# Decode and prompt tails of a one-core decoder step: rounding of the first chunk weights and merge weight steps moved in the written order

## The chip, the cores and the metric

The kernel runs on one core of a Trainium2 chip. The metric is the device time of one execution in microseconds. The engines are TensorE (PE; its weight loads are listed as PEld), VectorE (DVE), ScalarE (ACT), GpSimd (POOL) and SyncE (SP), which issues DMAs. They run side by side and wait for each other through semaphores. A "stage" of this kernel ends with a barrier of all engines.

## What is computed

One layer of a hybrid decoder, on a prompt of 256 tokens and on 8 sequences that decode 4 tokens each over a paged cache of 2048 rows. Cut to what matters here:

```
z   = RMSNorm(x) @ w_in                      # q, k, v, forget, branch gates, merge gates
NSA = gate_c * compressed(MLP of 32-row chunks) + gate_s * selected blocks + gate_w * window
FoX = softmax(q k + sum of log forget gates) v
h   = x + W_out( sigmoid(gA) * (W_oA NSA) + sigmoid(gB) * (W_oB FoX) )
y   = h + W_down( gelu(conv3(RMSNorm(h) W_up)) * (RMSNorm(h) W_gate) )
```

The chunk MLP needs weights `cmp_w1` (for k and v); the merge needs the gate columns gA and gB of `w_in`, in 8 groups of 128 columns, and `w_o`.

## The kernel before

All of it is float32. The large products are made of three passes with rounded halves: a "high" half, written by ScalarE (`split_high`, L249), a "low" half, the rest, written by VectorE (`split_low`, L254), and then high*high, low*high, high*low on TensorE (L261 to L263). A split is thus a ScalarE copy, then a VectorE subtraction that waits for it, then the products.

The stages in order are tokens, projection, prompt attention, compress (chunk MLP), decode, merge and FFN. Two places matter.

**The tail of the prompt stage** (`stage_prompt`, L752). Twelve units (four of selected and four of window attention, in turns, then four of FoX; U = 12) pass through scores, exponentials, `turn` (transposes of the probabilities, L902), copies out of PSUM (`take_turned`, VectorE L1029 for the first tile and ScalarE L960 for the second) and `values` (L925). `values(m)` waits for both copies of unit m, and for a FoX unit also for ScalarE's copy of the rows before it (`fox_rows_out`, L968). The loops run with lags: `turn` two steps and `values` three steps behind the scores. In this tail the kernel also prepares the next stage: TensorE transposes the first chunk rows (`chunks.turn(0, ...)`, L1105), ScalarE writes the high half of the first two eighths of the k chunk weights (`first_weights`), and VectorE their low halves, behind its last copy.

**The end of the decode stage** (`stage_decode`, L1573). The order of all work is one list of steps, `decode_steps()`, written out by hand; every engine runs through the same list and does what each step has for it. A `vals` step of job fox multiplies one block of gathered value rows (L1902, 8 products of 512 columns), one of job nsa the selected values of one sequence (L1868, L1871); `fold` sums slots (L1878 and L1907), `merge` scales them on VectorE (ending with L2147 for nsa, L2157 for fox), `out` transposes the result (L1764) and VectorE takes it (L2179, L2174). The rows come from the paged cache through GpSimd's indirect DMAs into a ring of 8 slots; a slot's next gather waits until its last user is done. Between these stand steps for the merge stage, which would have nothing else to wait for:

- `split(n)`: the halves of merge weights, n = 0 and 1 for the gate column groups `gates1` and `gates`, n = 2 for `w_o`.
- `branch(i)`: the halves of the prompt's NSA and FoX rows.
- `gates(n, x)`: the products of gate group n for branch x, 24 products of 288 columns (L261 to L263). `gates(0, x)` write PSUM banks 0 and 1, `gates(1, 0)` bank 4, which FoX logits used, `gates(1, 1)` bank 5, which holds the NSA sums until their merge.

When `gates(0, 1)` is done, GpSimd issues the load of a third gate group into the place of `gates1`, and ScalarE rounds it after its list. SyncE loads `w_o` when the last user of ring slot 5, the selected values of sequence 2, is done.

In the prompt stage this work is placed so:

```
if n == U + T_LAG - 1:                     # PE, n = 13: before turn(11)
    pe.wait_ge(neg, 4 * U)
...
    chunks.turn(0, lambda k, x: c.ps[x])
if n >= U + PV_LAG - EARLY:                # ACT, n = 13 and 14, last in each round
    first_weights(n - U - PV_LAG + EARLY)
for q in range(EARLY):                     # DVE, behind its loop
    dve.wait_ge(w_high, q + 1)
```

Of the kernel before, what the change touches and what calls it, by code (L numbers as in the profile page):

```python
# [751 lines left out]
def stage_prompt(c, z, chunks):  # L752


    nc, d = c.nc, c.d
# [4 lines left out]
    with c.stage() as ctx:  # L760
# [109 lines left out]
        def _(pe):  # L870
# [58 lines left out]
            for n in range(U + PV_LAG):  # L929
                if n < U:  # L930
                    scores(n)
                if n == 1:
                    cumulate()
                if n == T_LAG:
                    pe.wait_ge(cum_out, 2)
                if n == U + T_LAG - 1:
                    pe.wait_ge(neg, 4 * U)
                    for b in range(2):
                        pe.wait_ge(chunks.raw_in[b], 16)
                    chunks.turn(0, lambda k, x: c.ps[x])  # L940
                if T_LAG <= n < U + T_LAG:
                    turn(n - T_LAG)
                if n >= PV_LAG:
                    values(n - PV_LAG)

        @block.scalar
        def _(act):
# [25 lines left out]
            for n in range(U + PV_LAG):  # L973
                if n < U:
                    exponentials(n)
                if T_LAG <= n < U + T_LAG:
                    take_turned(n - T_LAG)
                if n >= N + PV_LAG:
                    fox_rows_out(n - N - PV_LAG)
                if n >= U + PV_LAG - EARLY:  # L980
                    first_weights(n - U - PV_LAG + EARLY)

        @block.vector
        def _(dve):
# [40 lines left out]
            def take_turned(m):  # L1025
# [2 lines left out]
                    dve.wait_ge(pv, m - 1)  # L1028
                nc.vector.tensor_copy(pT[m % 2][:, :, 0, :], c.ps[3][:, 0:2 * P].rearrange("p (j n) -> p j n", j=2)).then_inc(copied[0], 1)  # L1029

            def nsa_rows_out(r):
                dve.wait_ge(pv, 2 * r + 2)
                to = slice(r % 2 * HD, (r % 2 + 1) * HD)
# [5 lines left out]
            for n in range(U + T_LAG):  # L1039
# [4 lines left out]
                if n == 1:  # L1044
                    dve.wait_ge(cum_ready, 1)
                    nc.vector.tensor_copy(cq[:, :, :], c.ps[3][:, 0:2 * NH].rearrange("p (t h) -> p t h", t=QT)).then_inc(cum_out, 1)
                    nc.vector.tensor_scalar(neg_cq[:, :, :], c.ps[3][:, 0:2 * NH].rearrange("p (t h) -> p t h", t=QT), -1.0, None, ALU.mult).then_inc(cum_out, 1)
                if n >= T_LAG:
                    take_turned(n - T_LAG)
                if 1 <= n <= U:  # L1050
                    shares(n - 1)
                    normalise(n - 1)
                if 4 <= n < 4 + N and n % 2 == 0:
                    nsa_rows_out((n - 4) // 2)
            for q in range(EARLY):
                dve.wait_ge(w_high, q + 1)
                split_low(nc, chunks.eighths(chunks.w1l[0], q), chunks.eighths(chunks.w1[0], q), chunks.eighths(chunks.w1h, q))


ND = DB * NCH  # L1060
# [73 lines left out]
EARLY = 2  # L1134
# [343 lines left out]
def decode_steps():  # L1478
# [30 lines left out]
              + fold("fox", 0, 3) + select(1, 5))  # L1509
    end = (vals(1, 0) + merge("fox", 0) + probs(1, 3, 4) + nsa(1, 1) + out("fox", 0) + vals(1, 1) + probs(1, 0) + nsa(1, 2) + vals(1, 2) + nsa(1, 3) + vals(1, 3)  # L1510
           + nsa(1, 4) + vals(1, 4) + fold("fox", 1, 0) + nsa_probs(1, 0, 1) + vals(1, 5) + exps("sel", 1, 0, 1, 2) + nsa_probs(1, 2) + vals(1, 6) + exps("sel", 1, 3, 4)
           + nsa_probs(1, 3, 4) + vals(1, 7) + nsa_probs(1, 5, 6) + vals(1, 8) + fold("fox", 1, 1) + nsa_probs(1, 7) + branch(0) + nsa_vals(1, 0) + vals(1, 9)
           + split(0) + branch(1) + nsa_vals(1, 1) + vals(1, 10) + nsa_vals(1, 2) + gates(0, 0) + vals(1, 11) + nsa_vals(1, 3) + fold("nsa", 1, 0) + merge("nsa", 1)
           + gates(0, 1) + vals(1, 12) + out("nsa", 1) + fold("fox", 1, 2) + vals(1, 13) + split(1) + vals(1, 14) + gates(1, 0) + vals(1, 15) + fold("fox", 1, 3) + merge("fox", 1)
           + split(2) + gates(1, 1) + out("fox", 1))
    return start + middle + end


# [1444 lines left out]
```

## Time and profile before

| | |
|---|---|
| median of 3 runs | 906.74 us (906.27 to 909.92) |
| the profiled execution | 905.39 us, of which the span of the trace is 903.3 us |
| PE busy | 832.6 us, 92% of the span |
| DVE, ACT, POOL busy | 509.8 us (56%), 366.7 us (41%), 177.9 us (20%) |
| mean granted TensorE clock | 0.969 |
| HBM traffic | 188.09 MB read, 7.64 MB written |
| prompt stage ends, compress starts | 163.9 us, 164.7 us |
| decode ends, merge starts | 548.6 us, 549.5 us |

The busy shares are averages over stages with different limits. In the chain that ended last nearly all is TensorE (products of L261 to L263), since the last stage is bound by it; it doesn't tell what holds the earlier stages, for which the timelines are read.

### The profile page before, as it was taken

The page shows a single profiled execution, that of the slowest core. Times are in us where ns is not written, and L with a number is a line of the kernel's source. Part 1 is how long each engine was busy: PE and PEld are TensorE (multiplying, and loading weights), DVE is VectorE, ACT ScalarE, POOL GpSimd, SP SyncE. Part 2 cuts the span into 40 slices and gives each one's busy share as a digit, 9 for nine tenths or more (in the row PEclk, how much of TensorE's full clock was granted, in tenths as well). Part 3 has the DMA queues.
Part 4 walks back from the last instruction along what each step waited for, and adds up shares of the span by engine and source line. Part 5 has one row for each costly group of instructions (what it writes and reads, how often), then busy time and mean ns, then how long its engine had stood idle before and what let it go on. Part 6 is the DMA issues. An engine that isn't in the chain of part 4 may idle for free. (4 is left out here: it accounts for less than half of the span.)

```text
span 903.3 us, 18508 instructions
## 1 busy us (share of the span) xinstructions
PE 832.6 (92%) x7475; PEld 685.2 (76%) x7475; DVE 509.8 (56%) x970; ACT 366.7 (41%) x660; POOL 177.9 (20%) x274
## 2 busy tenths in 40 slices
PE   3899888899999999999998688999889999999997
PEld 3899756789889876656554357996589889989885
DVE  5477568433435677734566335646656655656654
ACT  4346655433334244632234403535154334444432
POOL 1000177200230033343443510000011100101100
PEclk9999869999999999999999899999989999999999
DMA  6453196752236299999999996954064445554412
GB/s 216 151 173 141 32 302 245 146 193 95 95 137 232 100 402 358 329 391 408 419 416 396 400 342 182 267 208 153 1 233 140 141 139 174 191 188 143 139 46 62
DMA packets 90785, 192.57 MB, mean 213 GB/s; under 512 B 7482, under 2 KB 68826, under 8 KB 78202
## 3 DMA queue, kind: packets, MB, share of 16 engines
q1 hardware_dynamic: 75020, 84.57, 30.4%
q0 software_dynamic: 15408, 106.04, 30.4%
q8 instruction: 51, 0.84, 0.4%
q10 hardware_dynamic: 288, 0.97, 0.3%
q14 instruction: 18, 0.15, 0.0%
HBM read 188.09 MB, written 7.64 MB: 217 GB/s over the span
## 5 line engine op out<-in xcount | busy, mean ns | idle before, releaser
L1729 PEld LDWEIGHTS banks<-consts_base,stream_rows 128*128 128x128 f32 x672 | 73.2, 141 | 33.9 <-issue 26.9
L1968 ACT ACTIVATE keys_turned<-banks 128x512 f32<-128x512 f32 x94 | 55.0, 597 | 98.2 <-PE banks L1729 90.9
L261 PE MATMUL banks<-tokens_turned_high,w_gates_high 128*128 128x288 f32 x288 | 86.6, 301 | 3.5 <-PEq L194 2.3
L1729 PE MATMUL banks<-consts_base,stream_rows 128*128 128x128 f32 x672 | 82.7, 276 | 7.4 <-DVE fox_probs_turned L1959 2.6
L262 PE MATMUL banks<-tokens_turned_low,w_gates_high 128*128 128x288 f32 x288 | 85.4, 297 | 0.0
L263 PE MATMUL banks<-tokens_turned_high,w_gates_low 128*128 128x288 f32 x272 | 81.8, 301 | 0.0
L1262 PE MATMUL banks<-chunks_turned_high,cmp_w_high 64*128 64x256 f32 (+1 forms) x512 | 77.2, 295 | 2.6 <-ACT cmp_hidden L1356 2.6
L1262 PE MATMUL banks<-chunks_turned_low,cmp_w_high 64*128 64x256 f32 (+1 forms) x512 | 73.9, 282 | 0.0
L1949 DVE COPY keys_turned<-banks 128x512 f32<-128x512 f32 x74 | 50.3, 690 | 32.9 <-PE banks L1729 28.2
L254 DVE TENSOR_TENSOR chunks_turned_low<-banks,chunks_turned_high 128x512 fp32r<-128x512 f32 x64 | 41.1, 685 | 41.2 <-ACT chunks_turned_high L249 41.2
L249 ACT ACTIVATE chunks_turned_high<-banks 128x512 fp32r<-128x512 f32 x64 | 34.8, 596 | 67.8 <-PE banks L1105 65.7
L261 PEld LDWEIGHTS banks<-tokens_turned_high,w_gates_high 128*128 128x128 f32 x288 | 55.3, 192 | 6.1 <-issue 3.5
L261 PE MATMUL banks<-tokens_turned_high,w_up_gate_high 128*128 128x288 f32 x192 | 58.0, 302 | 0.0
L263 PE MATMUL banks<-tokens_turned_high,w_up_gate_low 128*128 128x288 f32 x192 | 57.1, 297 | 0.0
L1262 PEld LDWEIGHTS banks<-chunks_turned_high,cmp_w_high 64*128 64x128 f32 x512 | 49.4, 187 | 9.7 <-issue 6.1
L262 PE MATMUL banks<-tokens_turned_low,w_up_gate_high 128*128 128x288 f32 x192 | 56.7, 295 | 0.0
L262 PEld LDWEIGHTS banks<-tokens_turned_low,w_gates_high 128*128 128x128 f32 x288 | 55.7, 194 | 0.4
L2784 POOL COPY conv_new_state<-up_turned 128x2 f32 (+1 forms) x24 | 16.4, 684 | 200.5 <-ACT up_turned L2750 200.5
L263 PEld LDWEIGHTS banks<-tokens_turned_high,w_gates_low 128*128 128x128 f32 x272 | 52.0, 191 | 0.0
L1262 PEld LDWEIGHTS banks<-chunks_turned_low,cmp_w_high 64*128 64x128 f32 x512 | 49.5, 187 | 0.0
L1564 POOL DMA_INDIRECT stream_rows<-in_cache_fox_k,fox_row x32 | 30.8, 963 | 87.9 <-PE banks L1729 39.6
L261 PE MATMUL banks<-w_in_high,tokens_turned_high 128*128 128x356 f32 x128 | 43.6, 341 | 3.3 <-DVE w_in_low L254 3.3
(454 smaller groups left out, 2096.4 us busy)
## 6 DMA issues: line engine op xcount, KB each, us to landing
w_up_gate<-in_w_up SPq DMA_DIRECT2D x12, 1024.0 KB, 7.5
w_up_gate<-in_w_gate SPq DMA_DIRECT2D x12, 1024.0 KB, 9.9
w_down<-in_w_down SPq DMA_DIRECT2D x12, 1024.0 KB, 5.1
w_in_slot<-in_w_in SPq DMA_DIRECT2D x7, 1424.0 KB, 7.3
w_gates<-in_w_in SPq DMA_DIRECT2D x10, 512.0 KB, 7.1
cmp_w_k<-in_cmp_w_k SPq DMA_DIRECT2D x4, 512.0 KB
cmp_w_v<-in_cmp_w_v SPq DMA_DIRECT2D x4, 512.0 KB
stream_rows<-in_state_win_k SPq DMA_DIRECT2D x8, 256.0 KB, 8.0
```

What stands on the lines that cost most here:

```text
L249: return nc.scalar.activation(high, x, ACT.Copy)
L254: return nc.vector.tensor_tensor(low, x, high.bitcast(F32), ALU.subtract)
L261: nc.tensor.matmul(out, lh, rh, start=start, stop=False, **kw)
L262: nc.tensor.matmul(out, lh, rl, start=False, stop=False, **kw)
L263: return nc.tensor.matmul(out, ll, rh, start=False, stop=stop, **kw)
L1262: ins = nc.tensor.matmul(c.ps[4 + g][:, 0:w], x[rows, half * CS + 4 * q + i, :], y[k % 2][rows, i, src], start=(q + i + half + part == 0), ...
L1564: c.nc.gpsimd.indirect_dma_start(c.stream[r][:, :], None, table, bass.IndirectOffsetOnAxis(ap=rows, axis=0)).then_inc(c.ring_in[r], 16)
L1729: ins = nc.tensor.transpose(bank(t)[:, q * P:(q + 1) * P], src, ident)
L1949: copy(kT[kbuf[step]][:, x, :], bank(t)).then_inc(copied[e], 1)
L1968: copy = lambda a, b: nc.scalar.activation(a, b, ACT.Copy)
L2784: nc.gpsimd.tensor_copy(dst[:, :, 0:2], ue[f][:, SEQ:SEQ + 2].unsqueeze(1))
```

## The change

The change moves work in the written order; no instruction is added or taken away. In the prompt stage ScalarE's two high halves of chunk weights move one and two rounds up, ahead of its copies; VectorE's two low halves go around its last copy out of PSUM instead of behind it; TensorE's transposes of the first chunk rows go from before `turn(11)` to between `values(10)` and `values(11)`. In the decode list, `split(0)` and `split(1)` come before `branch(0)` and `branch(1)`, the four `gates` steps move up between the value steps (two of them by three value steps, the last ahead of the last three FoX value blocks), and `split(2)` comes behind the last merge.

```diff
--- before.py
+++ after.py
@@ -933,13 +933,13 @@
                     cumulate()
                 if n == T_LAG:
                     pe.wait_ge(cum_out, 2)
-                if n == U + T_LAG - 1:
+                if T_LAG <= n < U + T_LAG:
+                    turn(n - T_LAG)
+                if n == U + PV_LAG - 1:
                     pe.wait_ge(neg, 4 * U)
                     for b in range(2):
                         pe.wait_ge(chunks.raw_in[b], 16)
                     chunks.turn(0, lambda k, x: c.ps[x])
-                if T_LAG <= n < U + T_LAG:
-                    turn(n - T_LAG)
                 if n >= PV_LAG:
                     values(n - PV_LAG)
 
@@ -977,8 +977,8 @@
                     take_turned(n - T_LAG)
                 if n >= N + PV_LAG:
                     fox_rows_out(n - N - PV_LAG)
-                if n >= U + PV_LAG - EARLY:
-                    first_weights(n - U - PV_LAG + EARLY)
+                if U <= n < U + EARLY:
+                    first_weights(n - U)
 
         @block.vector
         def _(dve):
@@ -1028,6 +1028,10 @@
                     dve.wait_ge(pv, m - 1)
                 nc.vector.tensor_copy(pT[m % 2][:, :, 0, :], c.ps[3][:, 0:2 * P].rearrange("p (j n) -> p j n", j=2)).then_inc(copied[0], 1)
 
+            def low_weights(q):
+                dve.wait_ge(w_high, q + 1)
+                split_low(nc, chunks.eighths(chunks.w1l[0], q), chunks.eighths(chunks.w1[0], q), chunks.eighths(chunks.w1h, q))
+
             def nsa_rows_out(r):
                 dve.wait_ge(pv, 2 * r + 2)
                 to = slice(r % 2 * HD, (r % 2 + 1) * HD)
@@ -1045,16 +1049,17 @@
                     dve.wait_ge(cum_ready, 1)
                     nc.vector.tensor_copy(cq[:, :, :], c.ps[3][:, 0:2 * NH].rearrange("p (t h) -> p t h", t=QT)).then_inc(cum_out, 1)
                     nc.vector.tensor_scalar(neg_cq[:, :, :], c.ps[3][:, 0:2 * NH].rearrange("p (t h) -> p t h", t=QT), -1.0, None, ALU.mult).then_inc(cum_out, 1)
+                if n == U + T_LAG - 1:
+                    low_weights(0)
                 if n >= T_LAG:
                     take_turned(n - T_LAG)
+                if n == U + T_LAG - 1:
+                    low_weights(1)
                 if 1 <= n <= U:
                     shares(n - 1)
                     normalise(n - 1)
                 if 4 <= n < 4 + N and n % 2 == 0:
                     nsa_rows_out((n - 4) // 2)
-            for q in range(EARLY):
-                dve.wait_ge(w_high, q + 1)
-                split_low(nc, chunks.eighths(chunks.w1l[0], q), chunks.eighths(chunks.w1[0], q), chunks.eighths(chunks.w1h, q))
 
 
 ND = DB * NCH
@@ -1509,10 +1514,10 @@
               + fold("fox", 0, 3) + select(1, 5))
     end = (vals(1, 0) + merge("fox", 0) + probs(1, 3, 4) + nsa(1, 1) + out("fox", 0) + vals(1, 1) + probs(1, 0) + nsa(1, 2) + vals(1, 2) + nsa(1, 3) + vals(1, 3)
            + nsa(1, 4) + vals(1, 4) + fold("fox", 1, 0) + nsa_probs(1, 0, 1) + vals(1, 5) + exps("sel", 1, 0, 1, 2) + nsa_probs(1, 2) + vals(1, 6) + exps("sel", 1, 3, 4)
-           + nsa_probs(1, 3, 4) + vals(1, 7) + nsa_probs(1, 5, 6) + vals(1, 8) + fold("fox", 1, 1) + nsa_probs(1, 7) + branch(0) + nsa_vals(1, 0) + vals(1, 9)
-           + split(0) + branch(1) + nsa_vals(1, 1) + vals(1, 10) + nsa_vals(1, 2) + gates(0, 0) + vals(1, 11) + nsa_vals(1, 3) + fold("nsa", 1, 0) + merge("nsa", 1)
-           + gates(0, 1) + vals(1, 12) + out("nsa", 1) + fold("fox", 1, 2) + vals(1, 13) + split(1) + vals(1, 14) + gates(1, 0) + vals(1, 15) + fold("fox", 1, 3) + merge("fox", 1)
-           + split(2) + gates(1, 1) + out("fox", 1))
+           + nsa_probs(1, 3, 4) + vals(1, 7) + nsa_probs(1, 5, 6) + vals(1, 8) + fold("fox", 1, 1) + nsa_probs(1, 7) + split(0) + nsa_vals(1, 0) + split(1) + vals(1, 9)
+           + gates(0, 0) + branch(0) + nsa_vals(1, 1) + vals(1, 10) + gates(0, 1) + branch(1) + nsa_vals(1, 2) + gates(1, 0) + vals(1, 11) + nsa_vals(1, 3) + fold("nsa", 1, 0)
+           + merge("nsa", 1) + vals(1, 12) + out("nsa", 1) + fold("fox", 1, 2) + gates(1, 1) + vals(1, 13) + vals(1, 14) + vals(1, 15) + fold("fox", 1, 3)
+           + merge("fox", 1) + split(2) + out("fox", 1))
     return start + middle + end
 
 
```

ScalarE, tail of the prompt stage (`prompt_probs_turned` is the copy of a unit's turned probabilities, `h_rows` the copy of a finished row pair, `cmp_w_high` the weight half). Before:

```order
L968 ACTIVATE h_rows<-banks 128x256
L960 ACTIVATE prompt_probs_turned<-banks 128x2x256
L968 ACTIVATE h_rows<-banks 128x256
L249 ACTIVATE cmp_w_high<-cmp_w_k 128x2x512
L968 ACTIVATE h_rows<-banks 128x256
L249 ACTIVATE cmp_w_high<-cmp_w_k 128x2x512
```

and with the change:

```order
L968 ACTIVATE h_rows<-banks 128x256
L249 ACTIVATE cmp_w_high<-cmp_w_k 128x2x512
L960 ACTIVATE prompt_probs_turned<-banks 128x2x256
L968 ACTIVATE h_rows<-banks 128x256
L249 ACTIVATE cmp_w_high<-cmp_w_k 128x2x512
L968 ACTIVATE h_rows<-banks 128x256
```

Both weight halves moved up by one copy or two; a row copy is now the engine's last work of the stage.

VectorE, the same tail, before and with the change:

```order
L1013 RECIPROCAL prompt_sums<-prompt_sums 128x4
L1023 TENSOR_TENSOR prompt_logits<-prompt_logits,prompt_sums 128x2x128
L1023 TENSOR_TENSOR prompt_logits<-prompt_logits,prompt_sums 128x2x256
L1029 COPY prompt_probs_turned<-banks 128x2x128
L254 TENSOR_TENSOR cmp_w_low_k<-cmp_w_k,cmp_w_high 128x2x512 x2
```

```order
L1013 RECIPROCAL prompt_sums<-prompt_sums 128x4
L1023 TENSOR_TENSOR prompt_logits<-prompt_logits,prompt_sums 128x2x128
L1023 TENSOR_TENSOR prompt_logits<-prompt_logits,prompt_sums 128x2x256
L254 TENSOR_TENSOR cmp_w_low_k<-cmp_w_k,cmp_w_high 128x2x512
L1029 COPY prompt_probs_turned<-banks 128x2x128
L254 TENSOR_TENSOR cmp_w_low_k<-cmp_w_k,cmp_w_high 128x2x512
```

The last copy out of PSUM, for which `values(11)` waits, now stands behind one of the two low halves.

TensorE, end of the decode, from the selected values of sequence 0 on (L1871 before and L1876 after are selected values, L1902 and L1907 a FoX value block, L261 and so on the gate products), before and with the change:

```order
L1871 MATMUL banks<-stream_rows,sel_logits 32x128 x16
L1902 MATMUL banks<-stream_rows,fox_probs_turned 32x512 x4
L1868 MATMUL banks<-sample_rows_kept,nsa_probs_turned 32x128
L1871 MATMUL banks<-stream_rows,sel_logits 32x128 x16
L1902 MATMUL banks<-stream_rows_66,fox_probs_turned 32x512 x4
L1868 MATMUL banks<-sample_rows_kept,nsa_probs_turned 32x128
L1871 MATMUL banks<-stream_rows_67,sel_logits 32x128 x16
L261 MATMUL banks<-tokens_turned_high,w_gates_high_early 128x288
```

```order
L1876 MATMUL banks<-stream_rows,sel_logits 32x128 x16
L1907 MATMUL banks<-stream_rows,fox_probs_turned 32x512 x4
L261 MATMUL banks<-tokens_turned_high,w_gates_high_early 128x288
L262 MATMUL banks<-tokens_turned_low,w_gates_high_early 128x288
L263 MATMUL banks<-tokens_turned_high,w_gates_low_early 128x288
```

The first 24 gate products now follow the FoX block that comes before the selected values of sequence 1; before, the first of them came after the selected values of sequence 2.

## Rows read from the trace of the kernel before

**Rows 1.** Timeline, VectorE, 155 to 164: start us, us, engine, line, op, operands, idle before

```profile
158.62 0.42 DVE L1029 COPY prompt_probs_turned<-banks 128x256 f32<-128x256 f32 x1 [0.99 <-PE banks L902]
...
162.63 1.23 DVE L254 TENSOR_TENSOR cmp_w_low_k<-cmp_w_k,cmp_w_high 128x1024 fp32r<-128x1024 f32 x1 [0.17 <-ACT cmp_w_high L249]
```

**Rows 2.** Timeline, ScalarE, the same stretch

```profile
157.39 0.39 ACT L968 ACTIVATE h_rows<-banks 128x256 f32<-128x256 f32 x1 [0.22 <-PE banks L925]
...
160.15 1.05 ACT L249 ACTIVATE cmp_w_high<-cmp_w_k 128x1024 fp32r<-128x1024 f32 x1
```

**Rows 3.** Timeline, TensorE, the same stretch

```profile
157.27 1.09 PE L1105 MATMUL banks<-consts_base,stream_rows 128*128 128x128 f32 x8
...
158.20 0.82 PE L902 MATMUL banks<-consts_base,prompt_logits 128*128 128x128 f32 x6
...
160.36 0.88 PE L925 MATMUL banks<-prompt_probs_turned,z 128*64 128x128 f32 x12 [0.53 <-issue]
```

**Rows 4.** Stretches: us; busy PE, PEld, DVE, ACT, POOL; clock, DMA share, GB/s

```profile
110.00:120.00 10.00, 7.63 (x36) 4.75 (x33) 6.00 (x37) 6.08 (x25) 7.91 (x9) 0.50 1.17 194
161.30:164.70 3.40, 0.00 (x0) 0.00 (x0) 2.39 (x2) 1.30 (x2) 0.00 (x0) 1.00 0.00 0
164.70:168.40 3.70, 3.63 (x26) 3.33 (x28) 2.58 (x4) 2.17 (x4) 1.63 (x9) 0.56 0.63 175
168.40:172.10 3.70, 3.70 (x50) 3.38 (x50) 0.00 (x0) 0.41 (x1) 0.57 (x2) 0.98 1.04 279
478.00:480.40 2.40, 0.14 (x2) 0.00 (x0) 2.26 (x7) 0.34 (x1) 0.00 (x0) 1.00 1.02 427
516.30:520.10 3.80, 3.57 (x42) 1.95 (x42) 0.29 (x1) 0.00 (x0) 0.94 (x1) 0.50 1.03 425
550.30:554.20 3.90, 3.76 (x17) 3.79 (x18) 2.20 (x1) 1.69 (x3) 0.18 (x1) 0.57 0.84 264
```

**Rows 5.** Timeline, TensorE, from 510 us to the end of the decode

```profile
510.35 1.07 PE L1902 MATMUL banks<-stream_rows,fox_probs_turned 128*32 128x512 f32 x8 [0.29 <-DMA stream_rows<-in_cache_fox_v,fox_row]
...
516.35 0.39 PE L1868 MATMUL banks<-sample_rows_kept,nsa_probs_turned 128*32 128x128 f32 x1 [4.93 <-DMA stream_rows<-in_cache_sel_v,eighth_row]
...
518.84 1.67 PE L1902 MATMUL banks<-stream_rows,fox_probs_turned 128*32 128x512 f32 x8 [0.18 <-DMA stream_rows<-in_cache_fox_v,fox_row]
...
521.32 0.27 PE L1868 MATMUL banks<-sample_rows_kept,nsa_probs_turned 128*32 128x128 f32 x1 [0.81 <-DMA stream_rows<-in_cache_sel_v,eighth_row]
...
528.53 0.43 PE L1878 MATMUL banks<-nsa_slot_sums,consts_base 128*32 128x128 f32 x8 [0.50 <-DVE nsa_slot_sums L2132]
...
537.51 0.40 PE L261 MATMUL banks<-tokens_turned_high,w_gates_high 128*128 128x288 f32 x1 [1.20 <-DVE w_gates_low_in_place L254]
...
542.76 1.04 PE L1907 MATMUL banks<-fox_slot_sums,consts_base 128*32 128x512 f32 x2 [0.81 <-DVE fox_slot_sums L2164]
...
547.02 0.60 PE L1764 MATMUL banks<-consts_base,fox_rows_out 128*128 128x128 f32 x4
```

**Rows 6.** Timeline, ScalarE, high halves of the merge weights in the decode

```profile
509.24 1.91 ACT L249 ACTIVATE w_gates_high_early<-w_gates_early 128x2048 fp32r<-128x2048 f32 x1
...
513.75 1.91 ACT L249 ACTIVATE w_gates_high<-w_gates 128x2048 fp32r<-128x2048 f32 x1 [1.66 <-DMA w_gates<-in_w_in]
...
540.26 1.06 ACT L249 ACTIVATE w_o_high<-w_o 128x1024 fp32r<-128x1024 f32 x1 [24.59 <-DMA w_o<-in_w_o_b]
```

**Rows 7.** Timeline, VectorE, end of the decode

```profile
511.18 2.29 DVE L254 TENSOR_TENSOR w_gates_low_early<-w_gates_early,w_gates_high_early 128x2048 fp32r<-128x2048 f32 x1 [0.37 <-ACT w_gates_high_early L249]
...
530.33 0.29 DVE L2147 TENSOR_TENSOR nsa_rows_out<-nsa_rows_out,consts_select 128x128 f32<-128x128 f32 x1
...
543.95 0.75 DVE L2157 SCALAR_TENSOR_TENSOR fox_rows_out<-banks,fox_sum_by_batch,consts_fox 128x512 f32<-128x512 f32 x1 [0.79 <-PE banks L1907]
...
544.61 1.21 DVE L254 TENSOR_TENSOR w_o_low_in_place<-w_o,w_o_high 128x1024 fp32r<-128x1024 f32 x1
...
547.66 0.89 DVE L2174 TENSOR_REDUCE fox_sample_out_turned<-banks 128x16 f32<-128x128 f32 x4 [1.83 <-PE banks L1764]
```

## The prediction, made before the changed kernel ran

> **What bounds the kernel now.** The chain that ended last is TensorE from 658 us on and shows nothing of the two places that change, so I read the timelines of each engine around them, then windows for the clock. At the end of the prompt stage the reader is to see who finishes last. TensorE ends its last `values` at 161.24 us [rows 3], VectorE its second low half at 163.86 [rows 1]: the barrier waits for the weight halves, and TensorE stands still for 3.4 us with nothing busy in it, after which the granted clock is 0.56 for 3.7 us, 26 products and transposes where the next 3.7 us hold 50 [rows 4]. At the end of the decode the reader is to see what each TensorE piece waited for. After the FoX block of 510.35 it waits 4.93 us for the rows of the selected values of sequence 1, then 0.18 and 0.81 us for two more gathers, 0.50 for VectorE's copy of a slot, 1.20 for the low half of `gates`, 0.81 for another slot copy [rows 5]: 8.4 us of idle time in 36 us, while gate products that need no gathered row stand behind those waits. In the long wait the clock falls, and from 516.3 to 520.1 it is 0.50, the low one of the two levels (1.2 GHz) [rows 4].
>
> **The change, part by part.** No instruction is added or removed, so every term is a wait that goes, comes or is covered.
>
> *A, prompt tail.* Step by step in the time of the old trace. ScalarE's row copy starts at 157.39; the first high half now follows it. A copy of this kind lets the next instruction start some 0.3 us after its own start, so the half runs from 157.7 and, at 1.05 us [rows 2], to 158.7. VectorE is free by then and writes the low half in 1.23 us [rows 1], 158.8 to 160.0; its last copy, 0.42 us, which stood at 158.62, now starts at 160.0 and ends at 160.4. TensorE runs `turn(11)` (0.82 us) and `values(10)` without the chunk transposes ahead of them, both done at about 159.2, then the chunk transposes (1.09 us) until 160.2, which cover the time in which `values(11)` waits for that late copy; `values(11)`, 0.88 us, ends at 161.3, where it ended before (161.24) [rows 3]. ScalarE's second high half follows its row copy at 159.6 and ends at 160.7, VectorE's second low half ends at 161.9, ScalarE's last row copy (0.39 us) at 161.7. So the stage ends at 161.9 instead of 163.86: **-2.0 us**. What if the cover fails: each us by which the VectorE copy is later moves `values(11)` and the last row copy, but not the low half, so 0.2 us is free and then it counts in full. The compress stage waits for nothing but this barrier and its own gathers, and the decode's gathers are issued by how far compress has come; the gain passes on.
>
> *B, the clock in compress.* TensorE's idle stretch shrinks from 3.5 us to the 0.9 us of the barrier and 0.6 before it, 1.5 us. The trace has both sides: after 3.4 idle us the clock was 0.56, in 2.4 us of near idleness (478.0 to 480.4) it stayed at 1.00 [rows 4]. 1.5 us is nearer to, and below, the second. The price of the low clock there is (1 - 0.56) x 3.7 = 1.6 us, and I take **-1.6 us**; the ends are 0 and -1.8.
>
> *C, decode end.* Again in the old trace's time, with gathers landing when they did (they are issued by the same releases, and the third gate group, now loaded about 9 us earlier, is queued by GpSimd behind all of them). `split(0)`: ScalarE's high half (1.91 us) takes the place of the branch half that stood just before 509.24, at 508.3 to 510.2 [rows 6]; the low half of 2.29 us [rows 7] ends at 512.6. TensorE, done with its FoX block at 511.4, waits 1.3 us, and `gates(0, 0)` runs 512.7 to 516.1. (A gate step lasts 3.3 us, from the end of the fold at about 543.75 to the transposes at 547.02 [rows 5].) The selected values of sequence 1 find their rows at 516.35, at full clock: 1.3 us, to 517.6. The next FoX block still has to wait for its rows at 518.84 and lasts 1.0. Then `gates(0, 1)` to 523.2, selected values 2 to 524.5 (rows there since 521.32), `gates(1, 0)` to 527.8; its weights, high half at 513.75 [rows 6], are ready by 518. FoX block 11 to 528.7, selected values 3 to 529.9, slot copy, fold at 530.4. The NSA merge takes VectorE from the fold to 530.62, 1.7 us after the fold ends (528.53 + 0.43) [rows 5, 7]; it used to lie beside `gates(0, 1)`, now beside one FoX block of 0.9 us, so 0.85 us of it is bare. Fold, `gates(1, 1)` to about 537.2, three FoX blocks to 539.9, slot copy with its 0.81 us, fold to 541.8. The FoX merge (0.2 us of latency and 0.75, as at 543.95 [rows 7]) used to lie beside `gates(1, 1)`; now 1.15 us of it is bare, and the transposes end at 543.6, where they ended at 547.62. The low half of `w_o` (1.21 us) stands between the merge and VectorE's last take (0.89): it delays that by 0.4, to 544.9 instead of 548.55. **-3.6 us**. The new idle time is 1.3 + 0.25 + 1.25 + 0.5 + 0.85 + 0.8 + 1.15 = 6.1 us for 8.4, and 1.6 us of low clock are gone; of these 3.9 the take gives back some 0.3. The bounds: if each step of the new list waited as little as the best of its kind, -5; if blocks 13 to 15 find their rows only when `w_o` landed (540.26, the end of the transfers [rows 6]), block 15 starts 1.3 us later, -2.3.
>
> *D, the loads.* SyncE issues `w_o` behind selected values 2, so 2 us later; it came in at 540.26, and ScalarE needs 1.06 us, so the low half is possible at 543.4 at the latest if the whole 2 us carry over, 0.6 behind its place. The third gate group's high half (1.91 us) follows on ScalarE and could end at 545.5. Taken at **0**, bound +0.6.
>
> *E, start of merge.* TensorE stood 2.82 us and the clock was 0.57 for 3.9 us after it [rows 4]. The gap stays 2.8 us, with 1.1 us of idle time just before; I take the same clock, 0; bounds -1.7 and +1.7, (1 - 0.57) x 3.9.
>
> Sum: -2.0 - 1.6 - 3.6 = -7.2 us. Against the profiled execution's 905.39 us that is 898.2. It lay 1.35 us below the median of the three runs (906.74), and the median is what is compared: **899.5 us**, 0.8% less. A measurement of this kernel can tell about 0.5%, 4.5 us, from no change.
>
> **Rivals.** *1. The clock falls in compress all the same.* The stretch before the barrier holds `turn`, the chunk transposes and two `values`, and compress opens with 8 transposes; if those don't keep the clock up, B is 0: -5.6 us, 901.1. For it: only 1.8 us of real products lie between 158.4 and the first chunk product. Against it: the wait at 478.0 lay between transposes of keys and the clock stayed at 1.00 [rows 4]. The Trainium skill ("TensorE: Matmul & The Clock Gate", Part 4: PE-mode transpose) says that a transpose does not count as busy for the gate. By that rule the time would be this rival's; the row at 478.0 speaks against it.
>
> *2. The transfers set the end of the decode.* The gathers are there only when they are there; work pulled ahead of them buys waiting. If block 15 and `w_o` are both late by the bounds of C and D, C is -2.3 and D +0.6: -5.3 with B, 901.4. For it: `w_o` took from 522.7 to 540.26 to arrive [rows 5, 6], so the queues were full to there. Against it: blocks 11 to 15 waited for no gather before.
>
> *3. Both, or a prompt tail in which the new order gains nothing:* -3.6 to -3.9 us, 903, within the 0.5%.
>
> *4. Slower: the clock goes down at the end of the decode and stays down.* The bare FoX merge and the barrier give TensorE 1.1 and 2.8 idle us with only 0.6 us of transposes between. If it stays low into the merge stage, whose products are dense, each us at 1.2 GHz costs half a us. From 110 to 120 us the trace shows 10 us at 0.50 while TensorE was 76% busy [rows 4], so a long low stretch is possible here. It decides from 14 us on, where it eats all 7.2; 24 us, about twice the row, give +5 us, 911.7. Against it: in the old merge stage the clock was back after one low stretch of 3.9 us.
>
> **How the numbers follow.** Forecast 0.53, rival 1 0.15, rival 2 0.16, rival 3 0.12, rival 4 0.04. Runs of one kernel spread by a few us (906.27 to 909.92). Under 902.2 (0.5% faster) lie nearly all of the forecast and two thirds of rivals 1 and 2: 0.73 faster. Same is the rest of them and rival 3, 0.23; slower 0.04. The range goes from 897.3 (the forecast with E at -1.7, and 0.5 of spread) to 903.6 (rival 3 and 0.5).
>
> **What would show it.** In the new profile compress starts 2.0 us earlier, near 162.7; VectorE still ends last in the prompt stage; TensorE's chunk transposes stand right before the last `values`; its first chunk products run at full clock; the wait of 4.93 us before the second selected values is under 1.5 us in two pieces with 24 gate products between; merge starts some 7 us earlier; after it all distances are the old ones. It is wrong if compress starts earlier but the decode's end doesn't follow, if FoX blocks 13 to 15 wait for gathers, or if a low clock stands where none was.

## The result: 900.7 us, close to the forecast number, with two of its three terms missing

The changed kernel took **900.74 us** (median of 5, 900.39 to 903.19) against 906.74 (5 runs, 903.92 to 909.92): ratio 0.9948, 95% interval 0.9929 to 0.9966. Timed again beside the experiments below it came to 0.9959 (0.9943 to 0.9975) and 0.9945 (0.9928 to 0.9962). So it is about 0.5% faster, 4.5 us on the mean of the three ratios; forecast were 7.2 us against the profiled execution. The profiled execution of after took 903.19 us (span 901.3) against 905.39 (span 903.3).

Two executions are never in step: after is 1.02 us late in the last transposes of the prompt already (156.24 against 155.22 us), before any changed instruction. So I compare distances. In the prompt's tail the new order is there, each step of TensorE, VectorE and ScalarE within 0.2 us of its place in the sum. Timelines of the profile after, VectorE and TensorE:

```profile
159.77 1.22 DVE L254 TENSOR_TENSOR cmp_w_low_k<-cmp_w_k,cmp_w_high 128x1024 fp32r<-128x1024 f32 x1 [1.13 <-ACT cmp_w_high L249]
160.91 0.41 DVE L1029 COPY prompt_probs_turned<-banks 128x256 f32<-128x256 f32 x1
161.57 1.28 DVE L254 TENSOR_TENSOR cmp_w_low_k<-cmp_w_k,cmp_w_high 128x1024 fp32r<-128x1024 f32 x1 [0.24 <-ACT cmp_w_high L249]
```

```profile
160.09 1.09 PE L1110 MATMUL banks<-consts_base,stream_rows 128*128 128x128 f32 x8
161.47 0.88 PE L925 MATMUL banks<-prompt_probs_turned,z 128*64 128x128 f32 x12 [0.29 <-DVE prompt_probs_turned L1029]
165.37 1.06 PE L1110 MATMUL banks<-consts_base,stream_rows 128*128 128x128 f32 x8 [3.01 <-PEq L194]
```

VectorE is done at 162.85, 1.0 us earlier than before and 2.0 once the 1.02 of lag are taken off. But the compress stage's first transposes stand at 165.37: counted from the prompt's last waiting transposes, after 9.13 us instead of 9.55. The gain is 0.4 us, not 2.0, and TensorE still idles for 3.0. The timelines of **GpSimd**, first before, then after, say why:

```profile
154.29 5.79 POOL L828 TENSOR_TENSOR h_rows<-h_rows,past_logf 128x32 f32<-128x32 f32 x15
160.15 0.25 POOL L829 TENSOR_TENSOR logf_of_partition<-h_rows,past_logf 128x32 f32<-128x32 f32 x1
164.73 0.12 POOL L1197 MEMSET prompt_cmp_k_by_group<- 128x32 f32 x1 [4.33 <-POOLq L194]
```

```profile
155.29 7.67 POOL L828 TENSOR_TENSOR h_rows<-h_rows,past_logf 128x32 f32<-128x32 f32 x15
163.04 0.25 POOL L829 TENSOR_TENSOR logf_of_partition<-h_rows,past_logf 128x32 f32<-128x32 f32 x1
165.32 0.12 POOL L1202 MEMSET prompt_cmp_k_by_group<- 128x32 f32 x1 [2.04 <-POOLq L194]
```

GpSimd sums the gates of the past tokens there, thirty additions in a chain. The same fifteen take 1.9 us longer and end behind VectorE. All of it is in two of them. The last seven additions as one group (durations in ns, least, median, most), and the second stalled one in a timeline of its own:

```profile
L828 POOL TENSOR_TENSOR h_rows<-h_rows,past_logf x7: 253/253/1282, 158.8 to 161.8; 128x32 f32<-128x32 f32 x7
```

```profile
161.85 1.11 POOL L828 TENSOR_TENSOR h_rows<-h_rows,past_logf 128x32 f32<-128x32 f32 x1
```

The first stalled one lasts from 159.82 to 161.10, beside VectorE's first low half (159.77 to 160.99). The second starts inside VectorE's second low half (161.57 to 162.85) and ends 0.1 us after it. Before, the second low half stood at 162.63 [rows 1] and the first right ahead of it, at 161.2, when GpSimd had finished (160.40). The old order has the same stall, only smaller: in its first fifteen additions one takes 0.58 us instead of 0.25. It starts beside VectorE's normalisation, which reads two SBUF tiles (L1023), and again ends 0.1 us behind it. GpSimd, then VectorE, before:

```profile
148.59 0.58 POOL L828 TENSOR_TENSOR h_rows<-h_rows,past_logf 128x32 f32<-128x32 f32 x1
```

```profile
148.32 0.74 DVE L1023 TENSOR_TENSOR prompt_logits<-prompt_logits,prompt_sums 128x512 f32<-128x512 f32 x1
```

And a stage that GpSimd ends is dear: its next instruction comes 2.04 us after its last, where the one behind VectorE's last came after 0.87 (163.86 to 164.73).

At the end of the decode the list did what was forecast. TensorE's timeline after:

```profile
511.49 1.07 PE L1907 MATMUL banks<-stream_rows,fox_probs_turned 128*32 128x512 f32 x8 [0.33 <-DMA stream_rows<-in_cache_fox_v,fox_row]
...
513.73 0.40 PE L261 MATMUL banks<-tokens_turned_high,w_gates_high_early 128*128 128x288 f32 x1 [1.17 <-DVE w_gates_low_early L254]
...
518.13 0.27 PE L1873 MATMUL banks<-sample_rows_kept,nsa_probs_turned 128*32 128x128 f32 x1 [0.94 <-DMA stream_rows<-in_cache_sel_v,eighth_row]
...
520.61 1.07 PE L1907 MATMUL banks<-stream_rows,fox_probs_turned 128*32 128x512 f32 x8 [1.23 <-DMA stream_rows<-in_cache_fox_v,fox_row]
...
532.23 0.42 PE L1883 MATMUL banks<-nsa_slot_sums,consts_base 128*32 128x128 f32 x8 [0.50 <-DVE nsa_slot_sums L2137]
...
534.46 0.30 PE L1769 MATMUL banks<-consts_base,nsa_rows_out 128*128 128x128 f32 x1 [0.95 <-DVE nsa_rows_out L2152]
...
539.04 2.78 PE L1907 MATMUL banks<-stream_rows,fox_probs_turned 128*32 128x512 f32 x24
...
542.64 1.05 PE L1912 MATMUL banks<-fox_slot_sums,consts_base 128*32 128x512 f32 x2 [0.81 <-DVE fox_slot_sums L2169]
...
544.72 0.63 PE L1769 MATMUL banks<-consts_base,fox_rows_out 128*128 128x128 f32 x4 [1.03 <-DVE fox_rows_out L2162]
```

The wait of 4.93 us [rows 5] is now 1.17 and 0.94 with a gate group between them, all others are within 0.2 us of the forecast, and the last three FoX blocks (24 products) waited for nothing. VectorE, after:

```profile
544.49 1.21 DVE L254 TENSOR_TENSOR w_o_low_in_place<-w_o,w_o_high 128x1024 fp32r<-128x1024 f32 x1
545.62 0.87 DVE L2179 TENSOR_REDUCE fox_sample_out_turned<-banks 128x16 f32<-128x128 f32 x4
```

The take ends at 546.49 instead of 548.55 [rows 7]. From the first selected values product of the second half (509.91; before 508.76) that is 36.6 us instead of 39.8. (This distance also depends on when an execution arrives there; see the table below.) The clock by stretches, columns as in [rows 4]: compress start, first gate group, the stretch that was at 0.50 before, merge start.

```profile
165.40:169.10 3.70, 3.32 (x28) 3.11 (x30) 2.48 (x4) 2.11 (x4) 1.54 (x9) 0.63 0.71 246
513.70:517.00 3.30, 3.27 (x24) 3.23 (x24) 0.28 (x2) 2.06 (x2) 1.72 (x2) 1.00 1.02 410
516.30:520.10 3.80, 2.14 (x41) 1.66 (x39) 3.21 (x2) 2.45 (x3) 0.39 (x1) 1.00 1.02 425
548.40:552.30 3.90, 3.90 (x17) 3.90 (x18) 2.05 (x1) 1.53 (x3) 0.02 (x1) 0.53 0.87 269
```

So the result seems to be C alone. Theory 1, which the experiments test: the prompt's new order gains nothing because VectorE's low halves stall GpSimd, whose exit then ends the stage, and its 3 us of idle drop the clock. Theory 2: A and B are there and an unlucky execution was profiled. Others stand with each run.

### The profile page after: what moved, and what is told of

It reads as the page before. It is cut to its first block and busy times, and to the rows that moved or that the text cites. A ratio compares the mean times of both kernels' runs of the same rounds, so it can differ in the third digit from the quotient of the medians.

```text
span 901.3 us, 18508 instructions
## 1 busy us (share of the span) xinstructions
PE 832.3 (92%) x7475; PEld 685.7 (76%) x7475; DVE 509.2 (56%) x970; ACT 366.3 (41%) x660; POOL 180.1 (20%) x274
## 3 DMA queue, kind: packets, MB, share of 16 engines
q1 hardware_dynamic: 75020, 84.57, 30.4%
## 5 line engine op out<-in xcount | busy, mean ns | idle before, releaser
L261 PE MATMUL banks<-tokens_turned_high,w_gates_high 128*128 128x288 f32 x288 | 86.5, 300 | 2.3 <-PEq L194 2.3
L261 PEld LDWEIGHTS banks<-tokens_turned_high,w_gates_high 128*128 128x128 f32 x288 | 55.3, 192 | 4.2 <-issue 3.7
L261 PE MATMUL banks<-tokens_turned_high,w_up_gate_high 128*128 128x288 f32 x192 | 58.0, 302 | 0.0
L1569 POOL DMA_INDIRECT stream_rows<-in_cache_fox_k,fox_row x32 | 30.8, 961 | 88.2 <-PE banks L1734 39.9
L261 PE MATMUL banks<-w_in_high,tokens_turned_high 128*128 128x356 f32 x128 | 44.0, 344 | 3.5 <-DVE w_in_low L254 3.5
```

What stands on the lines that cost most here:

```text
L261: nc.tensor.matmul(out, lh, rh, start=start, stop=False, **kw)
L1569: c.nc.gpsimd.indirect_dma_start(c.stream[r][:, :], None, table, bass.IndirectOffsetOnAxis(ap=rows, axis=0)).then_inc(c.ring_in[r], 16)
```

## The experiments

**The change taken apart.** `e1_repeat` is the changed kernel; `e2_prompt_only` has the new tail of the prompt and the old list; `e3_decode_only` the reverse. The edit is a swap of the last part of the list:

```diff
# e2_prompt_only, against the changed kernel
-... + nsa_probs(1, 7) + split(0) + nsa_vals(1, 0) + split(1) + vals(1, 9) + gates(0, 0) + branch(0) + ...
+... + nsa_probs(1, 7) + branch(0) + nsa_vals(1, 0) + vals(1, 9) + split(0) + branch(1) + ...
```

> The changed kernel once more, beside the three that take it apart. Both theories: 0.993 to 0.997 of the kernel before, some 901 us. If its profile again shows GpSimd last in the prompt's tail, its fifteen-addition groups near 7.7 us (5.79 before) with two additions over 1 us beside VectorE's two low halves, that is a property of the kernel and not of one execution. Rival (it was a chance of the one execution): GpSimd's two groups take 5.8 us each and the first compress transposes start 0.9 us after VectorE's last low half.

> The prompt's part of the change alone, the decode's list as before. Theory 1 (the low halves between the row copies stop GpSimd's additions, GpSimd ends the stage with an exit of some 2 us, and TensorE's idle of 3 us lets the clock fall all the same): the compress stage starts within 0.5 us of before, its clock falls to 0.56 as before, and the time is 0 to 1.0 us below the kernel before. Theory 2 (my forecast of terms A and B was right and the profile was a slow execution): 3 to 4 us below the kernel before.

> The decode list's part alone, the prompt's tail as before. Theory 1: nearly the whole gain of the change is here, 3.0 to 4.0 us below the kernel before; the last combination by the branch weights ends some 3.2 us earlier against the decode's own start, and the stretch in which TensorE ran at 0.56 before the last value steps is gone. Theory 2: it gives 3.6 us, and the whole change 7 us, so that the sum with the prompt part differs by 3 to 4 us.

Measured, against the kernel before (906.01 us): 0.9959 (0.9943 to 0.9975); **1.0002** (0.9985 to 1.002); **0.9962** (0.9947 to 0.9977). The prompt's part is worth nothing, the list 3.4 us, and they add up to the change. Theory 2 is out. GpSimd's second fifteen, from the profiles of e1, e2 and e3:

```profile
154.02 7.67 POOL L828 TENSOR_TENSOR h_rows<-h_rows,past_logf 128x32 f32<-128x32 f32 x15
```

```profile
155.03 7.67 POOL L828 TENSOR_TENSOR h_rows<-h_rows,past_logf 128x32 f32<-128x32 f32 x15
```

```profile
153.48 5.78 POOL L828 TENSOR_TENSOR h_rows<-h_rows,past_logf 128x32 f32<-128x32 f32 x15
```

The stall goes with the prompt's part, to a hundredth of a us.

**Take GpSimd out of the way.** `e4_spread_sums` makes the sums a generator and takes additions from it in the waits of GpSimd's loop:

```diff
+            sums = past_sums()
             for m in range(N):
                 normalise(m)
...
                 if m >= 5:
                     fox_bias_second(m - 5)
+                for _ in range({2: 5, 3: 2, 4: 1, 5: 3, 6: 7}.get(m, 0)):
+                    next(sums)
             fox_bias_second(NR - 1)
-            for half in range(2):
-                past_sums(half)
+            for _ in sums:
+                pass
```

> The changed kernel with GpSimd's thirty small additions of the past gates spread over the waits of its loop in the prompt, so that it is done some 8 us before the stage's end. Theory 1: each addition takes 0.25 us, VectorE is last, the compress stage starts 0.9 us after its last low half, 1.5 to 2.0 us earlier than in the changed kernel; TensorE's idle there falls from 3.0 to some 1.5 us and the clock stays at 1.00 (1.6 us more): 2 to 4 us below the changed kernel, 0.991 of the kernel before or less. Rival A (the clock falls in the compress stage whatever the idle, since transposes keep nothing up): the stage starts 1.5 to 2 us earlier, the clock still falls to 0.56: 1.5 to 2 us below the changed kernel. Rival B (the end of the stage is not set by GpSimd but by something of a fixed length behind TensorE): no change, within 0.5 us of the changed kernel.

Measured: 912.04 us, 1.006 (1.004 to 1.008), some 9 us above the changed kernel. A mistake of mine; GpSimd's timeline:

```profile
136.04 0.13 POOL L827 MEMSET h_rows<- 128x32 f32 x1 [10.03 <-DMA past_logf<-in_cache_fox_logf,eighth_row]
```

The past gates land only at 136 us. The first additions waited for them, with the prompt's own work queued behind. Still, one thing can be read. TensorE's timeline, and windows after it:

```profile
173.06 1.06 PE L1116 MATMUL banks<-consts_base,stream_rows 128*128 128x128 f32 x8 [1.66 <-PEq L194]
```

```profile
173.00:176.00 3.00, 2.55 (x31) 2.38 (x33) 2.33 (x4) 2.17 (x4) 1.64 (x9) 1.00 0.64 204
176.00:179.00 3.00, 3.00 (x40) 2.68 (x38) 0.16 (x1) 0.09 (x1) 0.57 (x2) 1.00 1.01 322
```

With 1.66 us of idle ahead of the stage the clock stays at 1.00. That speaks for B's mechanism and against rival A. This profile alone is weak evidence, since its clock had just been at 0.50 in the tail (166 to 168 us); e5 below has no such stretch.

**The same, at the right time.** `e5_late_sums` takes `{5: 3, 6: 6}`, nine additions after 138 us; `e6_late_sums_before` does so in the kernel before.

> The changed kernel with nine of GpSimd's thirty additions put into the waits of its loop after 138 us, when the past gates have landed (in e4_spread_sums they landed at 136.0 and GpSimd waited 10.0 us for them, with the whole prompt behind it); twenty-one stay at the end and are done by some 156 us, before VectorE's first low half. Theory 1 (shared stall, GpSimd's exit, then the clock): every addition takes 0.25 us, TensorE's idle before the compress stage is 1.5 to 1.7 us instead of 3.0, the clock stays at 1.00 in its first 6 us, and the time is 2.5 to 3.5 us below the changed kernel's, 0.992 to 0.993 of the kernel before. Rival (the start of the compress stage is made up for by the decode's transfers, which land when they land): the stage starts as early, but the last combination by the branch weights ends as late as in the changed kernel, and the time is within 0.7 us of it.

> The kernel before with the same nine additions moved, as the control. There VectorE ends the stage and GpSimd is done 3.4 us ahead of it, so all theories say: TensorE's idle stays 3.5 us, the clock falls to 0.56 in the compress stage, and the time is within 0.7 us of the kernel before. If it gains over 1.5 us, the moved additions have a worth of their own, and e5_late_sums shows nothing about the change.

Measured: e5 900.75 us, 0.9944 (0.9923 to 0.9966); e6 907.57, 1.0015 (1.0002 to 1.0029). Timelines of e5, GpSimd, VectorE, TensorE, and the window from the start of compress:

```profile
150.68 5.83 POOL L829 TENSOR_TENSOR h_rows<-h_rows,past_logf 128x32 f32<-128x32 f32 x15
156.59 0.40 POOL L831 TENSOR_TENSOR logf_of_partition<-h_rows,past_logf 128x32 f32<-128x32 f32 x1
```

```profile
160.47 1.23 DVE L254 TENSOR_TENSOR cmp_w_low_k<-cmp_w_k,cmp_w_high 128x1024 fp32r<-128x1024 f32 x1 [0.24 <-ACT cmp_w_high L249]
```

```profile
162.56 1.06 PE L1116 MATMUL banks<-consts_base,stream_rows 128*128 128x128 f32 x8 [1.30 <-PEq L194]
```

```profile
162.60:166.30 3.70, 3.32 (x44) 3.11 (x46) 2.48 (x4) 2.10 (x4) 1.54 (x9) 1.00 0.65 187
```

In the trace A has come in full and B nearly: VectorE last, 0.86 us to the next stage, 1.3 us idle, full clock, 44 products in the window where the changed kernel had 28. The control keeps 3.48 us of idle and a clock of 0.57. It came out 1.4 us slower, more than expected; its traces show the same distances as before, and I have no cause for it. Of the time, only about 1.4 us against `e1_repeat` (0.9944 and 0.9959, other rounds) are seen, less than the 2.5 to 3.5 expected. Two more sets of runs went to that.

> The changed kernel, on the same chip and in the same rounds as the next two, since e1_repeat and e5_late_sums were timed in different ones. 0.9945 to 0.996 of the kernel before.

> The kernel of e5_late_sums again, beside the changed kernel. Theory 1: the 2.7 us by which its last combination ended earlier in the profiles (542.8 against 545.5 us; the compress stage starts 1.5 us earlier and runs at a clock of 1.00 instead of 0.70 and 0.73 in its first six) come out in the medians: 2 to 3 us below e9_repeat. Rival (the two profiles were unlike executions, and the 2 us between the medians are chance): within 0.7 us of e9_repeat.

> The kernel of e2_prompt_only (the prompt's part alone, the decode's list as before) with GpSimd's nine additions moved as in e5_late_sums. Theory 1: from the prompt's last transposes to the first activation of the compress stage it takes 26.6 us as in e5_late_sums and e10_late_sums, 3.2 less than the 29.8 before, and the time is 2.5 to 3.5 us below the kernel before, 0.996 to 0.9975. Rival (the decode's transfers set its end, and what the prompt gains is waited away in front of them): the same 26.6 us, but the last value steps wait longer for their rows, the last combination ends within 1.5 us of before, and the time is 0 to 1.5 us below the kernel before.

Measured: e9 901.74 us, 0.9945 (0.9928 to 0.9962); e10 900.27, 0.9935 (0.9918 to 0.9952); e12 904.43, **0.9968** (0.9954 to 0.9981), beside e2's 1.0002. Distances out of all profiles, in us:

| kernel | prompt's last waiting transposes to compress | compress to its first `cmp_hidden` | compress to the second half's selected values | from these to the end of the take | ratio |
|---|---|---|---|---|---|
| before | 9.55 | 20.2 | 344.0 | 39.8 | 1 |
| changed (and e1, e9) | 9.13, 9.12, 9.12 | 20.4, 20.5, 20.5 | 344.5, 346.6*, 347.0* | 36.6, 34.9, 34.2 | 0.995 |
| e2, prompt part | 9.13 | 20.4 | 344.1 | 39.9 | 1.0002 |
| e3, list | 9.50 | 20.2 | 348.8* | 34.2 | 0.9962 |
| e6, additions moved in before | 9.50 | 20.2 | 344.3 | 39.8 | 1.0015 |
| e5, e10, additions moved in changed | 7.42, 7.42 | 19.1, 19.1 | 345.5*, 343.0 | 34.7, 36.4 | 0.994 |
| e12, additions moved in e2 | 8.58 | 19.2 | 346.1* | 38.1 | 0.9968 |

The star marks profiles in which the clock fell near 480 us, in the middle of the decode, which this change doesn't touch. TensorE waits there for 2.3 us in every profile of the table. In the changed kernel's first profile the clock stayed up behind that wait, in e9, the same kernel, it fell. First after, then e9, each with a line of TensorE's timeline and a window with columns as in [rows 4]:

```profile
481.69 0.66 PE L1734 MATMUL banks<-consts_base,stream_rows 128*128 128x128 f32 x4 [2.29 <-DVE fox_probs_turned L1964]
483.00:486.00 3.00, 2.92 (x26) 1.57 (x27) 2.43 (x9) 0.09 (x1) 2.46 (x3) 1.00 1.02 426
```

```profile
481.09 0.66 PE L1734 MATMUL banks<-consts_base,stream_rows 128*128 128x128 f32 x4 [2.29 <-DVE fox_probs_turned L1964]
483.00:486.00 3.00, 3.00 (x17) 0.46 (x10) 1.55 (x4) 0.00 (x0) 1.86 (x2) 0.52 1.03 429
```

A starred profile comes to the second half 2 to 5 us later, and the part behind it is then about 2 us shorter. So that column has to be read like with like: 39.8 against 36.6 without the star, 38.1 against 34.2 to 34.9 with it. The list is worth 3.2 to 3.9 us either way.

With the old list, freeing GpSimd turns the prompt's part from nothing into 3.1 us (2.9 below before), as expected. (e12's profile is its longest execution. The clock was at 0.53 from 159 to 162 us, in the tail itself, hence 8.58, and fell near 480 too. From the prompt's last waiting transposes to the end of the take it needs 392.7 us for 393.3 before, so this gain rests on the medians and is not seen in full in the trace.) With the new list it gives 0.9 and 1.4 us in the two pairs, each uncertain by over 2, which excludes neither 0 nor 3. One place to look is TensorE's waits for transfers in the profile of e10:

```profile
516.22 0.27 PE L1879 MATMUL banks<-sample_rows_kept,nsa_probs_turned 128*32 128x128 f32 x1 [0.62 <-DMA stream_rows<-in_cache_sel_v,eighth_row]
...
518.54 1.07 PE L1913 MATMUL banks<-stream_rows,fox_probs_turned 128*32 128x512 f32 x8 [1.06 <-DMA stream_rows<-in_cache_fox_v,fox_row]
```

From the first gate product to the end of the take, e9, e3, e5 and e1 need 30.4, 30.4, 30.9 and 31.1 us; e10 and the changed kernel's profile 32.6 and 32.8, with 1.7 and 2.2 us of such waits. The two slow ones are the two without the star, and one of them has none of the prompt's gain. So these waits go with the clock near 480 us and don't show that the prompt's gain is waited out. From the prompt's last waiting transposes to the end of the take, e10 needs 386.9 us and e5 387.7, where the three profiles of the changed kernel need 390.3 to 390.6: the traces keep 2.6 to 3.7 us. Why the medians show only 0.9 and 1.4 stays open.

**Which part of the list.** `e7_last_gates_early` moves only the last gate group in the old list; `e8_early_groups_only` is the new list with that group left behind the last value step, both with the old prompt tail; `e11_late_sums_tail` is e10 with the list of e8.

```diff
# e7, against the kernel before
-... + out("nsa", 1) + fold("fox", 1, 2) + vals(1, 13) + split(1) + ... + split(2) + gates(1, 1) + out("fox", 1))
+... + out("nsa", 1) + fold("fox", 1, 2) + gates(1, 1) + vals(1, 13) + split(1) + ... + split(2) + out("fox", 1))
# e8, against the changed list
-... + fold("fox", 1, 2) + gates(1, 1) + vals(1, 13) + ... + merge("fox", 1) + split(2) + out("fox", 1))
+... + fold("fox", 1, 2) + vals(1, 13) + ... + merge("fox", 1) + split(2) + gates(1, 1) + out("fox", 1))
```

> The kernel before with one move alone: the last gate group (gates(1, 1)) from behind the last value step to ahead of value step 13. Theory 1 (work behind the last transfer counts in full, work ahead of it counts where TensorE waits for a transfer anyway): the group of 3.2 us leaves the tail but stands ahead of value steps 13 to 15 which did not wait, so it takes the place of nothing by itself; within 0.7 us of the kernel before. Rival (the tail behind the last value step is what sets the end, since value steps 13 to 15 wait for their rows): 2 to 3.5 us below the kernel before.

> The changed decode list on the kernel before, but with the last gate group left behind the last value step: the two weight splits and three gate groups early, among the value steps that wait for transfers. Theory 1: nearly all of e3_decode_only's gain of 2.8 us is here, 2 to 3.5 us below the kernel before, since the 4.9 us wait for a transfer takes the first group. Rival (the last group's place is what gains): within 0.7 us of the kernel before.

> The kernel of e10_late_sums with the last gate group left behind the last value step, as in e8_early_groups_only. Theory 1 (that group hides beside VectorE's steps of the last fold when it stands there, and stands in the open ahead of value step 13, but then covers the wait for the last rows): within 0.7 us of e10_late_sums. Rival (the move of the last group is worth its own 3.2 us): 2 us or more above it.

Measured: e7 911.76 us, 1.0067 (1.0043 to 1.0092); e8 901.97, **0.9955** (0.9938 to 0.9973); e11 901.06, 0.9935 (0.9916 to 0.9954), as e10. TensorE in e7, then in e8:

```profile
539.90 0.40 PE L261 MATMUL banks<-tokens_turned_high,w_gates_high 128*128 128x288 f32 x1 [2.91 <-DVE w_gates_low_in_place L254]
...
552.46 0.63 PE L1764 MATMUL banks<-consts_base,fox_rows_out 128*128 128x128 f32 x4 [1.03 <-DVE fox_rows_out L2157]
```

```profile
537.87 1.06 PE L1902 MATMUL banks<-stream_rows,fox_probs_turned 128*32 128x512 f32 x8 [1.48 <-DMA stream_rows<-in_cache_fox_v,fox_row]
```

e8 has as much of the gain as the whole list (e3, 0.9962), within the noise: two splits and three groups early are what the list is worth. The last group's place is indifferent there. Behind the last value step it covers VectorE's merge; ahead of step 13 it covers the 1.48 us that e8's last block waits for its rows. In e7 it does harm, and neither theory had it: I had moved the group ahead of the split that makes its weights. TensorE waits 2.91 us for the low half instead of 1.20, FoX blocks 13 and 14 stand behind that wait, and the merge is bare for 1.03. That is 2.7 us. The distance from the second half's selected values to the end of the take is 42.0 us for 39.8 before. Its profile is one of those whose clock fell near 480 us (it reached the second half's selected values 346.4 us after compress began, before 344.0), and the old list's other such profile, e12, has 38.1. So the trace shows 2.2 to 3.9 of the 6 us, and the rest stays open.

## Why the prediction was right, and where it was wrong

**The number** (899.5; 897.3 to 903.6) held. The sum under it did not: C came, A and B did not. Of the 7.2 us about 4.5 were there. That the number was met is in part luck: 3.6 us of the sum did not come, and the first measurement fell on the good side of its interval, with 6.0 us between its two medians and 3.3 and 5.0 between the next two pairs.

**A, -2.0: failed**, at "So the stage ends at 161.9" and "The compress stage waits for nothing but this barrier". I followed three engines; the barrier has more. GpSimd was at its sums until 160.40 in the old trace, 0.8 us ahead of the old low halves, and the new order put these exactly beside it. The steps of these three engines were right to 0.2 us. With GpSimd out of the way (e5, e10) the distance falls by 2.13 us: A was sized right and held back by work that I had not looked at. The Trainium skill ("SBUF — State Buffer", Who interferes with whom) has the rule: a VectorE instruction with two inputs in SBUF and a GpSimd instruction that reads SBUF exclude each other, and the later one waits in full. The rows agree: both stalled additions started inside a low half and ended 0.1 us after it, having lasted 1.28 and 1.11 instead of 0.25.

**B, -1.6: did not come**, since A did not shorten the idle stretch enough: 3.0 us of idle, 0.63 in the window. Its mechanism was right at this place: with 1.3 us (e5, e10), 1.5 (e12) and 1.7 (e4) the clock stays at 1.00, and compress needs 19.1 us to its first activation instead of 20.4. So B is worth 1.3, 0.3 less than priced. Rival 1 falls with that: the stretch ahead of the barrier and the start of compress have their transposes in e5 too. By the rule quoted with it (the Trainium skill, "TensorE: Matmul & The Clock Gate", Part 4: PE-mode transpose) the clock was to fall there as well; the window at 1.00 speaks against that use of it. But the row on which B and the answer to rival 1 leaned, the near idleness at 478.0 with the clock at 1.00, was only one of two outcomes: behind that same wait of 2.3 us the clock fell in eight of thirteen profiles (e4's is left out), among them e1 and e9, which are the changed kernel again. What carries B is e5, e10 and e11, not that row.

**C, -3.6: right.** `e3_decode_only` gives 3.4 (2.1 to 4.8), and the traces 3.2 to 3.9, read like with like. The waits of after, 1.17, 0.94, 1.23, 0.50, 0.95, 0.81 and 1.03, answer to the forecast 1.3, 0.25, 1.25, 0.5, 0.85, 0.8 and 1.15; the second is a transfer that landed later than I had assumed. But the part on `gates(1, 1)` adds nothing (e8). **Rival 2** is half right: the last blocks wait for nothing, the middle ones wait when TensorE comes early.

**D, 0: right.** The high half of `w_o` still waited for its load, and the low half, straight behind VectorE's merge, delayed the take by 0.3 us (545.62 for 544.72 + 0.63), within the 0.4 in C. **E, 0: right**: 0.53 for 3.9 us after, 0.57 before. After the change the clock is low already ahead of the merge (0.50 from 546.0 to 548.4), where TensorE stands still and it costs nothing. **Rival 4** fell: the clock is back at 1.00 within 3.9 us of the merge's start, as before. **Rival 3** names the outcome in the prompt ("gains nothing"), without its cause.

Of my tests, "compress starts 2.0 us earlier" failed and pointed at A at once, while "VectorE still ends last" was the one that should have been a step of the forecast.

## What to carry to other kernels

Before you shorten the engine that ends a stage last, list when every engine of that stage ends, GpSimd too, and what each needs to leave it: the gain reaches only to the second of them. When an instruction is moved in time, look at what now lies beside it on the engines that share something with it, not only at its own queue. Where a long wait for a transfer stands in a list, fill that wait; here it mattered little where the last group went, as long as it did not stand ahead of what it needed. And one profile's row on the clock is one draw: look at the same wait in several executions before a term rests on it.

## What the runs showed of the hardware

- A VectorE subtraction of two 128x1024 operands in SBUF (1.23 us) held up a GpSimd addition of 0.25 us until it was done, to 1.28 and 1.11 us, in all profiles of this order with the sums at their old place (7.67, 7.67, 7.67 and 7.66 us for the second fifteen; after, e1, e2, e9), and in none of the others (5.78 to 5.84; e4 apart, which splits the fifteen). A shorter one of two inputs (L1023, 0.74 us) held an addition to 0.58 us in the old order.
- When GpSimd did its last work last, the next stage began 2.04 us after it, against 0.81 to 0.87 us behind VectorE.
- TensorE's granted clock fell after 3.0 to 3.5 us without work ahead of the compress stage (nine profiles, 0.54 to 0.65 over the stage's first 3.7 us), and stayed at 1.00 after 1.3 to 1.7 (e4, e5, e10, e11, e12).
- Short idle times don't protect it everywhere: behind the same wait of 2.3 us near 480 us it fell in eight profiles and stayed in five, and in e12 it fell at 159 us, where TensorE's longest wait shortly before had been 1.38 us.
